# Residual additions one PSUM bank at a time, in column halves, at the output projection and behind the last expert of an encoder trunk; last gate's final three pieces bank by bank

## The reference, cut to what matters

```python
for i in range(DEPTH):                       # 2
    hn = rms_norm(h, norm_mix[i])
    if i % 2 == 0:
        h = h + attn_conv_mixer(hn, ...)     # ends in mix @ w_out, 1024 x 1024
        h = h + swiglu(rms_norm(h, norm_ffn[i]), ...)
    else:
        h = h + multiscale_pool_mixer(hn, ...)
        h = h + moe_swiglu(rms_norm(h, norm_ffn[i]), ...)   # top 2 of 8 experts
    gate = sigmoid(rms_norm(h, ple_norm[i]) @ ple_gate_w[i])
    h = h + gate * (p[i] @ ple_proj[i])
```

## Time and profile before

| | |
|---|---|
| median of 3 runs | 1369.61 us (1369.44, 1369.61, 1370.93) |
| the profiled execution's own time | 1370.8 us |
| its span | 1369.0 us |
| TensorE busy | 1337.6 us, 98% of the span |
| VectorE, ScalarE busy | 1159.4 us (85%), 1009.0 us (74%) |
| mean granted TensorE clock | 0.996 |

### The profile page before, as it was taken

How to read it: one execution, slowest core, us unless ns; L and a number is a source line. 1 busy time by engine, 2 the same in 40 slices (tenths; PEclk the granted TensorE clock), 3 DMA queues, 4 the chain that set the end, 5 groups by cost and what they waited for, 6 DMA issues and landing times.

```text
span 1369.0 us, 19138 instructions
## 1 busy us (share of the span) xinstructions
PE 1337.6 (98%) x6738; PEld 1129.1 (82%) x6738; DVE 1159.4 (85%) x1247; ACT 1009.0 (74%) x1187; POOL 56.8 (4%) x58
## 2 busy tenths in 40 slices
PE   7999999999899999999999999999999999999998
PEld 6868999987678888888888888888888888888886
DVE  6986555556799999999999999999999999999995
ACT  6866444445777888888788888878888787888874
POOL 1000000000160000000000000000000000001000
PEclk9999999999999999999999999999999999999999
DMA  9407753376289899999989999999999999999930
GB/s 350 159 1 282 287 185 124 124 272 220 78 333 394 304 394 396 396 339 396 395 339 394 396 397 337 396 394 339 394 396 396 337 396 395 394 393 398 400 127 33
DMA packets 178482, 427.02 MB, mean 312 GB/s; under 512 B 4096, under 2 KB 13568, under 8 KB 178432
## 3 DMA queue, kind: packets, MB, share of 16 engines
q1 hardware_dynamic: 173248, 412.10, 80.2%
q0 software_dynamic: 3168, 11.54, 2.2%
q10 hardware_dynamic: 2016, 2.72, 0.6%
HBM read 419.53 MB, written 6.82 MB: 311 GB/s over the span
## 4 chain that ended last, share of the span: by engine, by line
PE 91%; DVE 5%; ACT 3%; issue 1%; DMA 0%; SPq 0%; ACTq 0%; DVEq 0%
PE G L1348 19%; PE G L1350 19%; PE G L1349 18%; PE Y L1348 11%; PE Y L1350 11%; PE Y L1349 11%; PE G L1688 2%; DVE lo_ring L786 1%; DVE ring L846 1%; ACT xT_hi L501 1%; DMA ring<-in_w_in 0%; ACT hi_ring L465 0%; ACT tok L558 0%; DVE xT_lo L816 0%; ACT tok L494 0%
## 5 line engine op out<-in xcount | busy, mean ns | idle before, releaser
L786 DVE TENSOR_TENSOR lo_ring<-ring,hi_ring 128x1024 fp32r<-128x1024 f32 x692 | 842.4, 1230 | 143.0 <-ACT hi_ring L465 101.5
L465 ACT ACTIVATE hi_ring<-ring 128x1024 fp32r<-128x1024 f32 x692 | 732.5, 1061 | 250.7 <-PE G L1350 150.9
L1348 PE MATMUL G<-hi_ring,xT_hi 128*128 128x512 f32 x896 | 353.4, 394 | 2.5 <-DVE lo_ring L786 1.4
L1350 PE MATMUL G<-lo_ring,xT_hi 128*128 128x512 f32 x896 | 349.4, 390 | 0.0
L1349 PE MATMUL G<-hi_ring,xT_lo 128*128 128x512 f32 x896 | 348.7, 389 | 0.0
L1348 PE MATMUL Y<-hi_ring,mT_hi 128*128 128x512 f32 x568 | 223.9, 394 | 0.0
L1350 PE MATMUL Y<-lo_ring,mT_hi 128*128 128x512 f32 x568 | 221.4, 390 | 0.0
L1349 PE MATMUL Y<-hi_ring,mT_lo 128*128 128x512 f32 x568 | 221.1, 389 | 0.0
L1348 PEld LDWEIGHTS G<-hi_ring,xT_hi 128*128 128x128 f32 x896 | 168.3, 188 | 36.3 <-DVE lo_ring L786 1.8
L1350 PEld LDWEIGHTS G<-lo_ring,xT_hi 128*128 128x128 f32 x896 | 168.2, 188 | 35.6
L1349 PEld LDWEIGHTS G<-hi_ring,xT_lo 128*128 128x128 f32 x896 | 168.4, 188 | 33.6
(11 more groups left out here) (248 smaller groups left out, 953.2 us busy)
## 6 DMA issues: line engine op xcount, KB each, us to landing
ring<-in_moe_wg SPq DMA_DIRECT2D x56, 2048.0 KB, 11.7
ring<-in_moe_wu SPq DMA_DIRECT2D x56, 2048.0 KB, 12.8
ring<-in_moe_wd SPq DMA_DIRECT2D x56, 2048.0 KB, 12.5
ring<-in_ffn_wg SPq DMA_DIRECT2D x5, 2048.0 KB, 11.5
ring<-in_ffn_wu SPq DMA_DIRECT2D x5, 2048.0 KB, 10.0
ring<-in_ffn_wd SPq DMA_DIRECT2D x5, 2048.0 KB, 9.0
ring<-in_ple_gate_w SPq DMA_DIRECT2D x4, 2048.0 KB, 7.8
y_rows<-misc POOLq DMA_DIRECT2D x9, 512.0 KB, 6.7
```

The source lines that it names most:

```text
L465: act.activation(hi_ring[:, n % AHEAD, :], where, ACT.Copy).then_inc(hi_done, 1)
L786: dve.tensor_tensor(lo_ring[:, n % AHEAD, :], where, hi_ring[:, n % AHEAD, :].bitcast(F32), ALU.subtract).then_inc(lo_done, 1)
L1348: pe.matmul(dst, s_hi, m_hi, start=start, stop=False, skip_group_check=True)
L1350: return pe.matmul(dst, s_hi, m_lo, start=False, stop=stop, skip_group_check=True)
```

## The change

The output projection walks columns first: bank 2c+t instead of 2t+c (`out_rows`, `last_out_rows`), its last two pieces go bank by bank, and VectorE adds each bank when it is complete (four additions of 512 columns in place of two of 1024), raising `half_ready` for the first column half and `h_ready` for the second. The transposes of norm 1 wait by column half. The same is done behind the last expert: the spreading matmuls go c, then t, and raise `scat_mm` four times. There the projection piece is cut in two: half of the transposes, the tile t = 0 of the piece, the other half, t = 1. Two waits for all of `norm_lo` become one for each bank (norms 2 and 5). The last three gate pieces go bank by bank (two by token tile before). The last bank's sigmoid, product, addition and store are cut in two quarters. Two splits of pieces change their places: piece 25 on ScalarE goes behind `norm_hi(1)`, and piece XP + AHEAD on VectorE behind `norm_lo(5)`.

```diff
+HALVED = (1, 5)
+LAST_PARTS = ((0, 0, 512), (1, 0, 512), (2, 0, 512), (3, 0, 256), (3, 256, 512))
...
-        for t, c0, c1, n in ((0, 0, D, 2), (1, 0, 512, 3), (1, 512, D, 4)):
+        for t, c0, c1, n in ((0, 0, D, 2), (1, 0, 512, 3), (1, 512, 768, 4), (1, 768, D, 5)):
...
+        hi_upto(20 + AHEAD)
+        norm_hi(1, Y8)
         hi_upto(21 + AHEAD)
-        norm_hi(1, Y8)
         norm(1)
...
-        for b in range(2 * T):
+        for n, (b, c0, c1) in enumerate(LAST_PARTS):
...
-        def add_rows(i, use, end):
+        def add_halves(i, use, end):
+            for c in range(2):
+                for t in range(T):
+                    b = 2 * c + t
+                    dve.wait_ge(bank_done, 3 * use + b + 1) if b < 3 else dve.wait_ge(pe_piece, end)
+                    dve.tensor_tensor(h[:, t, c * 512:(c + 1) * 512], h[:, t, c * 512:(c + 1) * 512], Y[:, b, :],
+                                      ALU.add).then_inc(h_ready if c else half_ready, 1)
             dve.wait_ge(h_ready, T * (i + 1))
...
             last(XP - 1 + AHEAD)
-            for t in range(T):
-                dve.wait_ge(scat_mm, t + 1)
-                dve.wait_ge(pair_add, T + t + 1)
-                dve.scalar_tensor_tensor(out=h[:, t, :], in0=Y[:, 2 * t:2 * t + 2, :].rearrange("p b n -> p (b n)"),
-                                         scalar=last_gate[:, t:t + 1], in1=h[:, t, :], op0=ALU.mult, op1=ALU.add).then_inc(h_ready, 1)
+            for c in range(2):
+                for t in range(T):
+                    part = h[:, t, c * 512:(c + 1) * 512]
+                    dve.wait_ge(scat_mm, 2 * c + t + 1)
+                    dve.wait_ge(pair_add, T + t + 1)
+                    dve.scalar_tensor_tensor(out=part, in0=Y[:, 2 * c + t, :], scalar=last_gate[:, t:t + 1], in1=part,
+                                             op0=ALU.mult, op1=ALU.add).then_inc(h_ready if c else half_ready, 1)
+            norm_lo(5, Y8)
             last(XP + AHEAD)
-            norm_lo(5, Y8)
...
+        for n, (b, c0, c1) in enumerate(LAST_PARTS):
+            t, c = b // 2, slice((b % 2) * 512 + c0, (b % 2) * 512 + c1)
+            dve.wait_ge(sig_gate, 2 * T + n + 1)
+            link(dve.tensor_tensor(tok[:, t, c], tok[:, t, c], G[:, b, c0:c1], ALU.mult))
+            dve.tensor_tensor(h[:, t, c], h[:, t, c], tok[:, t, c], ALU.add).then_inc(gated, 1)
...
+        def norm_half(i, bank, half):
...
+                for k in range(half * KT // 2, (half + 1) * KT // 2):
+                    if i in HALVED:
+                        if half == 0 and t == 0 and k % 2 == 0:
+                            pe.wait_ge(half_ready, T * HALVED.index(i) + k // 2 + 1)
+                        if half and t == 0 and k == KT - 2:
+                            pe.wait_ge(h_ready, T * (i + 1))
+                    ins = pe.transpose(bank[:, k, t * P:(t + 1) * P], src[:, t, k * P:(k + 1) * P], ident)
...
-        def rows(n, s_hi, s_lo, bank, first, last):
+        def rows(n, s_hi, s_lo, bank, first, last, freed=None):
...
+                    if freed is not None:
+                        pe.wait_ge(nlo_done, freed + 2 * (2 * t + c + 1))
...
+        def last_out_rows(n, e):
+            for u in range(2):
+                pe.wait_ge(lo_done, n + u + 1)
+            for c in range(2):
+                for t in range(T):
+                    for u in range(2):
...
+                        if (c, t) == (1, T - 1):
+                            piece(n + u, ins)
+                    if (c, t) != (1, T - 1):
+                        ins.then_inc(bank_done, 1)
...
-            pe.wait_ge(nlo_done, KT * 3)
             for k in range(KT - 4):
-                rows(first + 2 + k, xT_hi[:, k, :], xT_lo[:, k, :], Y, k == 0, False)
+                rows(first + 2 + k, xT_hi[:, k, :], xT_lo[:, k, :], Y, k == 0, False, None if k else KT * 2)
...
+            for c in range(2):
+                for t in range(T):
+                    dst = Y[:, 2 * c + t, :]
+                    pe.matmul(dst, spread[:, t * P:(t + 1) * P], y_hi[c], start=True, stop=False)
+                    pe.matmul(dst, spread[:, t * P:(t + 1) * P], y_lo[c], start=False, stop=True).then_inc(scat_mm, 1)
             for t in range(T):
...
-            norm(5, Y8)
-            last_rows_of(XP + 1, pT_hi[1][:, 1], pT_lo[1][:, 1], G, False, True)
-            pe.wait_ge(nlo_done, KT * 6)
-            for k in range(KT - 2):
+                norm_half(5, Y8, t)
+                last_rows_of(XP + 1, pT_hi[1][:, 1], pT_lo[1][:, 1], G, False, True, (t,))
+            for k in range(KT - 3):
...
+            for u in range(3):
+                pe.wait_ge(last_lo, XP + KT - 1 + u - AHEAD + 1)
+            for b in range(2 * T):
+                t, c = b // 2, slice((b % 2) * 512, (b % 2 + 1) * 512)
+                for u in range(3):
...
+                if b < 2 * T - 1:
+                    ins.then_inc(bank_done, 1)
```

More of the change, by code:

```diff
@@ L945, in _ @@
         lo_upto(19 + AHEAD)
-        add_rows(1, 0, 22)
+        add_halves(1, 0, 22)
         norm_lo(1, Y8)
@@ L1020, in _ @@
         lo_upto(FIRST[g0 + 3] - 1)
-        gate(0)
+        gate()
         dve.wait_ge(gate_add, 2 * T)
@@ L1355, in unread @@
                 pe.matmul(bank, xT_hi[:, 0, 0:P], xT_hi[:, 0:2, :], start=True, stop=True)
+        def norm_half(i, bank, half):
+            src = h if i in RAW else tok
+            for t in range(T):
+                if i not in HALVED and i not in RAW:
+                    pe.wait_ge(tok_done, T * SCALED.index(i) + t + 1)
+                elif half or i not in HALVED + (4,):
+                    pe.wait_ge(h_ready, T * i + t + 1)
+                elif i == 4:
+                    pe.wait_ge(pooled, t + 1)
+                for k in range(half * KT // 2, (half + 1) * KT // 2):
[5 more added lines that the diff above has]
+                    ins = pe.transpose(bank[:, k, t * P:(t + 1) * P], src[:, t, k * P:(k + 1) * P], ident)
+                    if t == T - 1:
+                        ins.then_inc(tr_done, 1)
         def norm(i, bank=G8):
-            src = h if i in RAW else tok
             for half in range(2):
[L1363 to L1373, removed]
+                norm_half(i, bank, half)
         def cols_tokens(n0, pieces, dst, width):
@@ L1432, in bank_rows, with out_rows @@
                     ins.then_inc(bank_done, 1)
+        def out_rows(n, e, first):
+            pe.wait_ge(lo_done, n + 1)
+            w_hi, w_lo = hi_ring[:, n % AHEAD, :], lo_ring[:, n % AHEAD, :]
+            for c in range(2):
+                for t in range(T):
+                    ins = three(Y[:, 2 * c + t, :], mT_hi[:, e, t * P:(t + 1) * P], mT_lo[:, e, t * P:(t + 1) * P],
+                                w_hi[:, c * 512:(c + 1) * 512], w_lo[:, c * 512:(c + 1) * 512], first, False)
+            piece(n, ins)
+        def last_out_rows(n, e):
+            for u in range(2):
+                pe.wait_ge(lo_done, n + u + 1)
+            for c in range(2):
+                for t in range(T):
+                    for u in range(2):
+                        w_hi, w_lo = hi_ring[:, (n + u) % AHEAD, :], lo_ring[:, (n + u) % AHEAD, :]
+                        ins = three(Y[:, 2 * c + t, :], mT_hi[:, e + u, t * P:(t + 1) * P], mT_lo[:, e + u, t * P:(t + 1) * P],
+                                    w_hi[:, c * 512:(c + 1) * 512], w_lo[:, c * 512:(c + 1) * 512], False, u == 1)
+                        if (c, t) == (1, T - 1):
+                            piece(n + u, ins)
+                    if (c, t) != (1, T - 1):
+                        ins.then_inc(bank_done, 1)
         def last_rows(n, tiles, bank):
@@ L1537, in _ @@
         ins.then_inc(mean_mm, 1)
-        rows(14, mT_hi[:, 0, :], mT_lo[:, 0, :], Y, True, False)
+        out_rows(14, 0, True)
         pe.wait_ge(sq_done, 1)
@@ L1740, in last_transposes, with last_rows_of @@
             act_transposes().then_inc(last_at_mm, 1)
-        def last_rows_of(q, s_hi, s_lo, bank, first, last):
+        def last_rows_of(q, s_hi, s_lo, bank, first, last, tokens=range(T), freed=None):
             pe.wait_ge(last_lo, q - AHEAD + 1)
             w_hi, w_lo = hi_ring[:, q % AHEAD, :], lo_ring[:, q % AHEAD, :]
-            for t in range(T):
+            for t in tokens:
                 for c in range(2):
+                    if freed is not None:
+                        pe.wait_ge(nlo_done, freed + 2 * (2 * t + c + 1))
                     ins = three(bank[:, 2 * t + c, :], s_hi[:, t, :], s_lo[:, t, :],
                                 w_hi[:, c * 512:(c + 1) * 512], w_lo[:, c * 512:(c + 1) * 512], first, last)
-            ins.then_inc(last_piece, 1)
+                if t == T - 1:
+                    ins.then_inc(last_piece, 1)
         def last_expert(done):
@@ L1781, in last_expert @@
             pe.wait_ge(ylo_done, 2)
-            for t in range(T):
-                for c in range(2):
-                    dst = Y[:, 2 * t + c, :]
```

(5 more changed lines are left out.)

46 lines of the change are left out of this document (17 added, 29 removed).

## The result

| | before | after |
|---|---|---|
| median of 12 runs each | 1369.78 us | 1366.95 us |
| lowest to highest | 1369.44 to 1371.59 | 1364.86 to 1369.47 |
| profiled execution, own time | 1370.8 | 1367.19 |
| its span | 1369.0 | 1365.3 |

The ratio of after to before is 0.9977, 95% interval 0.9969 to 0.9985: 3.15 us less, between 2.1 and 4.2. The medians differ by 2.8 us and the two profiled spans by 3.7. The forecast was 1366.3 us in a range of 1365.2 to 1368.0, a gain of 3.31 us.

A forecast was written before the change was run, and what follows sets the result against it. TensorE, busy for 98% of the span, was taken to bound the kernel. Terms 1.09 + 0 + 1.69 - 0.05 + 0.58 + 0 = 3.31 us, taken from the 1369.61 us median, gave 1366.3 us, range 1365.2 to 1368.0.

The forecast's parts named there:

- Output projection: Output projection to first SwiGLU matmul: additions by bank let that matmul start at 121.47 instead of 122.56, gaining 1.09 us.
- First gate: Gate behind norm 2: TensorE starts 0.35 us sooner but waits for VectorE's last lo piece; gain 0, bounds 0 and 0.35.
- the low clock: First gate: a longer wait brings the clock dip in most runs, giving back 1.6 us, to 1367.9; chance 0.17.
- Behind the last expert: From the spreading matmuls to the last gate: first gate piece starts at 1340.1 against 1341.68, without a stalled entry; gain 1.69 us.
- Last three pieces: Last gate pieces: TensorE wants the last lo piece one piece earlier, a stall of 0 to 0.1 us, taken as 0.05.
- Tail: Behind TensorE's end: the last addition ends 2.24 us after it instead of 2.82, gaining 0.58 us by the order, not the quarters.
- Store: Last store, 128 KB instead of 256: bounds 0.5 us gained and 0.3 lost, taken as 0.
- From the trace to the median: The profiled execution's 1.2 us above the median was laid to a first-gate clock dip of 1.6 us, absent or short in the median run.
- a gain given back by the last gate's pieces: Last gate: ScalarE or VectorE sets the next piece and half of 1.69 us is lost, to 1367.1; chance 0.15.
- the slow end: Last gate: TensorE waits for the last lo piece and runs 36 matmuls at low clock, 1371.8 or 1375.9 us; chance 0.04.
- the additions were not hidden: The rival held that the additions were already mostly hidden, so that only the tail's gain shows, 1369.0 us; chance 0.04.
- the signs of being wrong: Last three pieces' first row idle above 0.2 us, longer norm 1 to norm 2, or low clock outside 333 to 338 us.

The follow-up runs named there:

- experiment 5: The kernel before with only the change at the output projection and norm 1; median 1369.76 us of 11 runs, ratio 0.9992.
- experiment 8: The changed kernel run again without any edit; median 1366.72 us of 6 runs, ratio to the kernel before 0.9972.
- experiments 1 and 7: Changed kernel, each executed once: with the last bank whole, 1369.26 us; with the last two pieces by token tile and the quarters kept, 1369.89 us.
- experiment 1: Changed kernel with the last bank in one part instead of quarters, bank order kept; executed once with the profiler, 1369.26 us.
- experiment 12: The kernel before run again without any edit; executed once with the profiler, 1371.42 us.
- experiments 9 and 11: Changed kernel with the bands' transfer on GpSimd's queue, median 1364.45 us, ratio 0.9957; the same plus pool weights scaled early, 1363.32 us, ratio 0.9953.

## Why the prediction was right, point by point

- **Output projection**: 1.09 us forecast, 1.10 measured, and 1.12 up to norm 2. That all of it travels to the end is not shown: the experts' stretch takes 0.2 to 0.4 us longer in most kernels with this projection, the one of experiment 5 too, a term that the sum does not have. The cover of the moved split was argued rightly and its price set too low (0.4 against 0.55): ScalarE does its pieces back to back, and the piece before ended later than I had counted. Bank by bank, pieces 20 and 21 both end with the last bank, so ScalarE starts on the piece before 0.49 us ahead of the first transpose (118.35) instead of 1.16 (117.87).
- **First gate**: 0 forecast, 0.08 measured at the last piece of the first bank in the first pair of traces, 0.77 in the second. The mechanism was right: the last piece starts 14.65 us behind ScalarE's first piece behind norm 2, whatever TensorE does. What I had wrong is that ScalarE's start stays where it was; it moves with one issue on its queue (experiment 8). The idle time grew by 0.57, not 0.35 us. What I called a rival, the low clock, was there in the trace after and not in the repeat. Of the eleven traces with this stall it followed in the four whose third piece had waited 0.41 to 1.01 us (before, after, experiments 1 and 7) and in none of the seven with 0 to 0.36. So a part of the gain can be given back where TensorE comes earlier to the same stall.
- **Behind the last expert**: 1.69 forecast to the last three pieces, 1.85 measured. The additions, the interleaved projection piece and the banks ran as computed, within 0.2 us each. The moved lo piece was counted as free, and is; it is also useless.
- **Last three pieces**: a stall of 0.05 forecast, 0.05 measured.
- **Tail**: 0.58 forecast, 0.61 measured. The quarters bring nothing on VectorE, in keeping with the Trainium skill's rule on small tiles (VectorE: DVE Perf Modes, TRN2 errata): 2.21 us against 2.16 without them in experiment 1. Where the order was by tile they cost 0.25 us (3.07 against 2.82).
- **Store**: 0 forecast, 0.26 measured, inside the bounds. This term of the sum was mis-sized.
- **From the trace to the median**: this step was half wrong. I explained the 1.2 us between the profiled execution and the median by the low clock at the first gate. The trace of before had it, but the upper group of times (1371 to 1372) has another cause: experiment 12 took 1371.42 without it, with the low level at the start. Three things varied from trace to trace: some 2 us at the start, 1.5 at the first gate's clock, and one issue on ScalarE's queue, whose 0.8 us reach the gate in the changed kernel. They are the likely reason, not one that single times can prove, why its times spread over 4.6 us. The medians show 2.8 us; the stretches behind norm 1's first transpose show 3.5 in one pair of traces and 4.4 in the other. That the forecast of 3.31 lies so near the measured 3.15 (2.1 to 4.2) is in part luck: the store and the first gate gave more than forecast, and the experts' stretch took some of it back.

The rivals: a gain given back by the last gate's pieces did not show, nor the slow end; the additions were not hidden. Of the signs of being wrong, one was drawn too narrowly: the granted clock is also below 1 between 360 and 380 us, in the kernel before as in the changed one (0.90 and 0.76, then 0.82 and 0.84, by stretches of 10 us), so it says nothing of the change.

## What to carry to other kernels

Where an engine waits for a result to be folded into the next stage's input, hand it over in the units in which the next stage reads it (here a PSUM bank by column halves, and a wait for each bank): at the two places and the end together it was worth 3.6 us of stretches (1.12 + 1.85 + 0.61), of which some 0.4 went again elsewhere, in a kernel in which TensorE was already busy nearly throughout. Before counting on it, look at what the freed engine meets next: in front of the first gate TensorE's earlier start was worth nothing in itself until five instructions of VectorE were moved out of the chain, and those brought 1.5 us, or 3.8 against a trace with the slow issue and the low clock. And compare kernels stretch by stretch between events of the traces; a difference of 0.1% that the times blur stands there to a few hundredths of a microsecond. Take two traces of each kernel before you do: here one trace alone would have put 0.8 us of a slow issue and 1.5 us of clock down to the edit.

## What the runs showed of the hardware that was not expected

- A transfer issue on ScalarE's queue that usually takes 0.45 us took 0.98 to 1.39 us in nine of the fourteen traces, one issue in each. In the kernel before it was the second of the pool scales in both traces, in the changed kernel the bands in one of two. Its length tells in the gate: in the kernel before, 1.35 us went with an idle time of 0.41 ahead of the third piece and the low clock, 1.21 us with 0.28 and none. What makes one issue slow is open; with the bands on another queue none was slow in the two traces taken (experiments 9 and 11; 0.49 us at most).
- The lower clock level behind the stalls of the first gate followed two waits, not the longer alone: 1.45 us by itself or with up to 0.36 us shortly before it did not bring it (0 of 7 traces), with 0.41 to 1.01 us it came each time (4 of 4). The waits between are those traces' own; no run set this distance on purpose.
- The granted clock reads 1.00 for the first 20 us in all fourteen traces, also in the seven where the distance of the matmuls (0.21 us against 0.12) speaks for the lower level.
